# Filler matmuls in two softmax attentions, and query blocks in ascending order in the top-k one

## The reference, cut to what matters

```python
# first block: four heads of 64, query blocks of 128
s_c = einsum(q, k_cmp) * scale      # 31 compressed keys
o_c = softmax(s_c, masked) @ v_cmp
s_s = einsum(q_rope, k_sel) * scale # selected blocks (here every causal key)
o_s = softmax(s_s, masked) @ v_sel
s_w = einsum(q_rope, k_win) * scale # window of 512
o_w = softmax(s_w, masked) @ v_win
o = g0 * o_c + g1 * o_s + g2 * o_w
s = einsum(q_mem, mem_k) * scale; o_mem = softmax(s) @ mem_v   # 256 memory keys

# second block: 8 index heads choose the keys, 16 heads attend
rel = relu(einsum(q_idx, k_idx))
score = einsum(w_idx, rel), masked causally
sel = top_k(score, 128)
logits = einsum(q, k[sel]) * scale; o = softmax(logits) @ v[sel]
```

## Time and profile before

| | |
|---|---|
| median of three timed runs | 2147.55 us (2138.83 to 2147.99) |
| the profiled execution's own time | 2135.49 us |
| its span, first to last instruction | 2133.3 us |
| mean granted TensorE clock | 0.864 |
| PE busy | 1923.1 us (90%) |
| PEld busy | 1519.7 us (71%) |
| DVE busy | 944.0 us (44%) |
| ACT busy | 843.1 us (40%) |
| POOL busy | 260.8 us (12%) |

### The profile page before, as it was taken

One profiled execution on the slowest core, in us unless ns is written; L12 is line 12 of the kernel. 1 busy time (PEld: TensorE's weight loads), 2 busy tenths in 40 slices (PEclk: granted clock), 3 DMA queues, 4 the chain that ended last, 5 costly groups with the idle time before them and its releaser, 6 DMA issues. The chain is left out here.

```text
span 2133.3 us, 31157 instructions
## 1 busy us (share of the span) xinstructions
PE 1923.1 (90%) x12332; PEld 1519.7 (71%) x12332; DVE 944.0 (44%) x1622; ACT 843.1 (40%) x1368; POOL 260.8 (12%) x209
## 2 busy tenths in 40 slices
PE   5999388879978888998799999979999889999997
PEld 4887188745547645677688888868888768888885
DVE  2343835472245578434433333345555443333233
ACT  4223245343333443333444442246555244343322
POOL 3000223110003250000200000022222030000000
PEclk9999579765569995557899999999999889999998
DMA  4321100000012110001122333322221113323321
GB/s 169 99 89 45 40 3 3 19 27 1 1 31 75 50 30 1 1 1 59 57 93 98 98 93 100 94 73 90 70 70 60 42 59 99 97 91 97 99 99 49
DMA packets 37760, 131.66 MB, mean 62 GB/s; under 512 B 4816, under 2 KB 5136, under 8 KB 37392
## 3 DMA queue, kind: packets, MB, share of 16 engines
q1 hardware_dynamic: 36784, 127.91, 18.8%
q10 hardware_dynamic: 864, 2.17, 0.3%
HBM read 127.17 MB, written 2.10 MB: 61 GB/s over the span
## 5 line engine op out<-in xcount | busy, mean ns | idle before, releaser
L138 DVE TENSOR_TENSOR big_parts<-ring,big_parts 128x1024 fp32r<-128x1024 f32 x164 | 205.2, 1253 | 525.9 <-ACT big_parts L133 525.9
L156 PE MATMUL bank<-h_parts,big_parts 128*128 128x512 f32 x960 | 381.7, 398 | 26.4 <-POOL y_parts L1391 17.6
L157 PE MATMUL bank<-y_parts,big_parts 128*128 128x512 f32 x960 | 377.9, 394 | 0.0
L158 PE MATMUL bank<-h_parts,big_parts 128*128 128x512 f32 x960 | 377.3, 393 | 0.0
L133 ACT ACTIVATE big_parts<-ring 128x1024 fp32r<-128x1024 f32 x164 | 173.7, 1061 | 287.7 <-PE bank L158 287.4
L156 PEld LDWEIGHTS bank<-h_parts,big_parts 128*128 128x128 f32 x960 | 182.7, 190 | 67.3 <-issue 28.6
L158 PEld LDWEIGHTS bank<-h_parts,big_parts 128*128 128x128 f32 x960 | 182.7, 190 | 38.3
L157 PEld LDWEIGHTS bank<-y_parts,big_parts 128*128 128x128 f32 x960 | 182.9, 190 | 37.1
L157 PE MATMUL bank<-y_parts,work_parts 128*128 128x512 f32 x456 | 180.5, 396 | 0.0
L138 DVE TENSOR_TENSOR work_parts<-ring,work_parts 128x1024 fp32r<-128x1024 f32 x65 | 79.4, 1224 | 165.3 <-ACT work_parts L133 165.3
L133 ACT ACTIVATE work_parts<-ring 128x1024 fp32r<-128x1024 f32 x65 | 68.7, 1060 | 205.6 <-PE bank L158 175.3
(11 more groups left out here) (398 smaller groups left out, 3072.9 us busy)
## 6 DMA issues: line engine op xcount, KB each, us to landing
ring<-in_wstream SPq DMA_DIRECT2D x229, 512.0 KB, 3.5
x<-in_xt SPq DMA_DIRECT2D x4, 512.0 KB, 7.8
out_t<-x SPq DMA_DIRECT2D x8, 256.0 KB, 2.0
work<-in_memt ACTq DMA_DIRECT2D x1, 1024.0 KB, 14.5
work<-in_cw SPq DMA_DIRECT2D x1, 1024.0 KB, 5.1
cst<-in_cst ACTq DMA_DIRECT2D x1, 704.0 KB, 7.9
cos<-in_reset SPq DMA_DIRECT2D x2, 256.0 KB, 2.7
big<-work SPq DMA_DIRECT2D x4, 128.0 KB, 4.2
```

What stands on the lines that cost most here:

```text
L138: dve.tensor_tensor(self.parts[:, self.place_of(n), 1, :, :], self.ring[:, n % RING, :, :], self.parts[:, self.place_of(n), 0, :, :].bitca ...
L156: pe.matmul(out, w[0], x[0], start=start, stop=False, skip_group_check=True)
L157: pe.matmul(out, w[0], x[1], start=False, stop=False, skip_group_check=True)
L158: return pe.matmul(out, w[1], x[0], start=False, stop=stop, skip_group_check=True)
```

## The change

Three edits. The helper `warm` issues matmuls of 256 columns instead of 512. `stage_nsa` passes a table that puts 12 fillers ahead of the transposes of unit 0 and one ahead of those of every other unit, 75 in all. `stage_dsa` passes one with 10 for unit 3, 2 for each of units 4 to 15, 6 for unit 16 and 1 for each after that, 87 in all, and takes `late` as (1, 2, 3) instead of (3, 2, 1). The result of a filler is used by nobody.

```diff
 def warm(c, pe, bank, n):
 
     for _ in range(n):
-        pe.matmul(bank[:, :], con(c, "ident"), c.cst[:, 0:4, :], start=True, stop=True)
+        pe.matmul(bank[:, 0:2 * P], con(c, "ident"), c.cst[:, 0:2, :], start=True, stop=True)
@@ stage_nsa
-    at = Attend(c, "na", units, 8576, 4, finishes)
+    fill = {n: 12 if n == 0 else 1 for n in range(len(units))}
+    at = Attend(c, "na", units, 8576, 4, finishes, fill)
@@ stage_dsa
-    late = (3, 2, 1)
+    late = (1, 2, 3)
@@
-    at = Attend(c, "da", units, 8 * T, 8, finishes)
+    fill = {n: 1 if n > 16 else 2 for n in range(4, len(units))} | {3: 10, 16: 6}
+    at = Attend(c, "da", units, 8 * T, 8, finishes, fill)
```

## The result

The changed kernel takes 2088.54 us (median of four runs, 2082.16 to 2095.18) against 2143.2 us of the kernel before in the same comparison. The ratio is 0.9745, 95% interval 0.9701 to 0.9788: faster by 2.5%, some 55 us. Forecast were 2079 us (2048 to 2112) and 60 us saved.

A forecast was written before the change was run, and what follows sets the result against it. Both attentions were taken as TensorE-bound at half clock. Terms -28 (first attention), -33 (top-k), +1.5 (index part), -1 (output transposes) sum to -60.5 us from 2135.5; plus 4 for scatter gives 2079 us, range 2048 to 2112.

The forecast's parts named there:

- The filler's price: Both attentions: a 256-column filler costs TensorE 0.46 us at the high clock, 0.92 at the low; upper bound 0.61.
- the factor: Both attentions: at the higher clock whole turns take 0.54 of their former time; bounds used 0.50 and 0.57.
- the forecast 28: First attention: 28 us saved by the higher clock after paying for 75 fillers; bounds 14 to 34.
- 33: Top-k attention: 33 us saved, 138.8 against 172.2 us, with 87 fillers and the new order; bounds 22 to 40.
- the 7.9 of the sum: Head of the first attention: the twelve fillers ahead of the first unit add 7.9 us.
- The order: Top-k attention: picks of q=1, 2, 3 moved beside the units of q=0, 1, 2; about 7 us by itself.
- The index part: Top-k stage's index matmuls, 256-column ones first: GpSimd contention moves to 256-wide VectorE steps, +1.5 us (-3 to +5).
- A: First attention: the twelve lift the clock, but it falls again in the light 31-key units; about 2173 us, chance 6%.
- B: First attention: the clock falls in each light group and returns in the heavy ones; about 2107 us, chance 8%.
- C: Both attentions: the clock lift never comes, so all 162 fillers cost 0.92 us; 2281 us, chance 2%.
- D: Both attentions: transposes don't count for the clock, so q=2 and q=3 fall back to 0.50; about 2193 us, chance 2%.
- E: Clock stays up, but VectorE and ScalarE take over sooner, losing 25 us of the gain; 2104 us, chance 8%.

The follow-up runs named there:

- the best version here: Against the changed kernel: first-attention fillers only at query block 0 and 31-key units, no top-k fillers for q=3; 2069.88 us, ratio 0.9653 to the kernel before.

## Why the prediction was right, and where it was off

**What bounds, and what the fillers do.** Right. Both stages were bound by TensorE at the low clock, the twelve and the ten lifted it, and the singles held it. Of the neighbours of this change, the one without singles gains nothing, the one with a quarter of the array loses 7%. The bet that the clock stays up through both stages had no row behind it when it was made, and held; the two groups of times with half-size fillers show how near the other outcome was.

**The filler's price and the factor: the terms that were mis-sized.** The sum has 3.25 x 0.54 + 0.46 = 2.22 us for a heavy turn of the first attention; it takes 2.31. By its start and the next one the filler takes 569.70 - 569.16 = 0.54 us of that, and the rest 1.77 of 3.25, just the factor 0.54. But without its filler the turn takes 1.83 us, not 1.77. Read so, the filler costs 0.48, near the 0.46 of the sum, and the factor is 0.56 where the sum has 0.54. The changed kernel shows only the two together, and either way the turn is 0.09 us longer than forecast. The weight loads show where the 0.05 us come from: behind a filler (first row, the changed kernel) the transposes' load starts 0.22 us ahead of them, without one (second row) only with them.

```profile
569.48 0.58 PEld L957 LDWEIGHTS bank<-cst,work 128*128 128x128 f32 x4
```

```profile
557.66 0.42 PEld L957 LDWEIGHTS bank<-cst,work 128*128 128x128 f32 x4 [0.33 <-ACT work L986]
```

Split by starts, the 0.08 us more on the 63 singles of the first attention are 5 us, on the 77 of the top-k one that follow its ten 6. With it the forecast 28 becomes 23 (measured 23.3), and 33 becomes 27 (measured 26.1 in the units). The twelve were a little cheaper than the 7.9 of the sum, 474.70 - 467.82 = 6.9 us from their start to the first transpose.

**The light units.** Not seen in the forecast: a 31-key turn gains next to nothing. It lasted 1.38 us and lasts 1.34 (the timeline's starts of its scores below, before and after), where the forecast's own terms give 1.38 x 0.54 + 0.46 = 1.21. Its own work is so short that the filler eats nearly the whole gain. That is the price of holding the clock for the others.

```profile
487.15 0.63 PE L947 MATMUL bank<-work,big 64*128 64x31 f32 x2
...
488.53 0.63 PE L947 MATMUL bank<-work,big 64*128 64x31 f32 x2
```

```profile
494.99 0.40 PE L947 MATMUL bank<-work,big 64*128 64x31 f32 x2
...
496.33 0.41 PE L947 MATMUL bank<-work,big 64*128 64x31 f32 x2
```

**The order.** Its working at the low clock was about right (7 us forecast, 5.5 in the units), and that q=2 would be even between TensorE and VectorE too. The starts 813.22, 845.82 and 879.79 us give 2.04 us a turn for q=1 and 2.12 for q=2, where 1.69 and 2.08 were forecast. The first is longer since its turns hold the six fillers and three of the double ones, eight fillers more than one a turn, so q=1 is TensorE's and not even.

```profile
813.22 0.42 DVE L999 CUSTOM_DVE_ANT_0 work<-bank,big 128x256 f32<-128x256 f32 x1 [0.56 <-DVE work L1963]
...
845.82 0.56 DVE L999 CUSTOM_DVE_ANT_0 work<-bank,big 128x384 f32<-128x384 f32 x1
...
879.79 0.69 DVE L999 CUSTOM_DVE_ANT_0 work<-bank,big 128x512 f32<-128x512 f32 x1 [0.57 <-PE bank L158]
```

**The index part.** +1.5 us forecast, -1.6 measured, within the bounds. It belongs to the order: 28.9 us with the order alone, 30.5 with the fillers alone. The timeline after shows what was missing before, VectorE's 256-wide steps (L1949) beside GpSimd's operations (L180), and 512-wide ones free of them; the last row is of before, 256-wide steps free of them.

```profile
754.63 11.15 POOL L180 TENSOR_TENSOR y_parts<-big,work_parts 128x512 fp32r<-128x512 f32 x8 [6.66 <-ACT work_parts L176]
754.93 9.73 DVE L1949 SCALAR_TENSOR_TENSOR work<-work 128x256 f32<-128x256 f32 x7 [0.50 <-ACT work L1922]
764.58 1.42 DVE L1946 TENSOR_SCALAR work<-work 128x384 f32<-128x384 f32 x1
...
772.60 0.48 DVE L1946 TENSOR_SCALAR work<-work 128x512 f32<-128x512 f32 x1
773.19 5.89 DVE L1949 SCALAR_TENSOR_TENSOR work<-work 128x512 f32<-128x512 f32 x7
```

```profile
794.84 4.02 DVE L1947 SCALAR_TENSOR_TENSOR work<-work 128x256 f32<-128x256 f32 x7
```

Beside GpSimd a 256-wide step takes 9.73 / 7 = 1.39 us, as long as one of GpSimd's operations (11.15 / 8 = 1.39), where a 512-wide one took 1.63. Free of it they take 4.02 / 7 = 0.57 and 5.89 / 7 = 0.84. So the contention adds 0.8 us to a step of either width, and moving it from the wide steps to the narrow ones gains nothing: VectorE's first eight steps take 10.5 us where they took 12.5, its last eight 6.5 where they took 4.5. The 1.6 us lie around them. The first step starts 1.6 us after the part's first matmul instead of 2.7, and the first pick, which this part includes, has 256 columns instead of 512, 0.6 us less.

**The rivals.** A, B, C and D did not occur. E was in part what happened to the size, but not its mechanism: TensorE, not VectorE, spent the difference. D's rule is refuted for these transposes by a kernel of its own.

**The median.** The 4 us added for the scatter were too few: the profiled execution before is among the fastest, and the medians of 7, 13 and 11 further runs of that kernel are 2143.6 to 2143.7 us, 8 above it. The 9.5 us between the forecast 2079 and the measured 2088.54 are these 4 and some 6 of the sum: the stages of the table gave 54.5 us where it had 60.5.

## What to carry to other kernels

When a stage keeps TensorE busy at the low clock, the first question is whether its own work could hold the high one; then a lift of full-size matmuls ahead, and single ones only in the turns that are too light, can pay: the best version here took a fifth (top-k) and a quarter (first) off the two stages. Take the fillers away group by group and watch the clock by windows: here those of 36 units of the first attention and of q=3 in the other stage were pure cost, 19 us. And time such a kernel several times before trusting it: half-size fillers gave about 2066 or 2191 us from the same program.

## What the runs showed of the hardware

- PE's busy share in the profile says nothing of the clock: 224.00 of 224 us busy at 0.50 with quarter-array fillers, 108.00 of 108 at 1.00 with full-size ones.
- f32 transposes of 128x128 as fillers lift the clock and, beside the attention's own work, hold it: 48 at the head, then 1.00 for 117 and for 135 us, in all 2090.59 us against 2088.54 with matmuls.
- The same turns ran at 0.50 for 138 us with TensorE never idle, and at 1.00 once it was lifted; with half-size fillers one program gave 2065 and 2067, or 2190 and 2193 us, from run to run.
- A filler's price depends on how it is read: 0.54 us by the starts, 0.48 by the turn without it, 0.43 by the stage without 36 of them.
- VectorE beside GpSimd: 1.39 us a step for 256 columns and 1.63 for 512, against 0.57 and 0.84 free of it. Beside GpSimd a step lasts as long as one of its operations: 1.39 us after, and 9.71 / 6 = 1.62 before.
